# A paged hybrid decoder step on one core: the order of work at the start of the expert stage

## The reference, cut to what matters

```python
        q = (tb @ wq).reshape(blk, PEER_HEADS, PEER_D_KEY)
        s1 = jnp.einsum('thd,hkd->thk', q[..., :half], keys[:, 0])
        s2 = jnp.einsum('thd,hkd->thk', q[..., half:], keys[:, 1])
        sc1, i1 = lax.top_k(s1, PEER_TOPK)
        sc2, i2 = lax.top_k(s2, PEER_TOPK)
...
        sc, sel = lax.top_k(cand, PEER_TOPK)
        idx = jnp.take_along_axis(cidx, sel, axis=-1)
        g = jax.nn.softmax(sc.astype(jnp.float32), axis=-1)
        act = jax.nn.gelu(jnp.einsum('thkd,td->thk', u[idx], tb), approximate=False)
        wgt = (g * act.astype(jnp.float32)).astype(tb.dtype)
        return jnp.einsum('thk,thkd->td', wgt, v[idx])
```

## Time and profile before

| what | value |
|---|---|
| median of 3 executions | 2105.01 us (2101.08 to 2106.8) |
| the profiled execution's own time | 2099.31 us |
| its span, first to last instruction | 2097.5 us |
| mean granted TensorE clock | 0.823 |
| TensorE busy | 1662.4 us, 79% |
| VectorE busy | 1446.4 us, 69% |
| ScalarE busy | 489.6 us, 23% |
| GpSimd busy | 676.2 us, 32% |
| read from HBM | 733.48 MB, 355 GB/s over the span |

### The profile page before, as it was taken

How to read it: one execution, slowest core, us unless ns; L and a number is a source line. 1 busy time by engine, 2 the same in 40 slices (tenths; PEclk the granted TensorE clock), 3 DMA queues, 4 the chain that set the end, 5 groups by cost and what they waited for, 6 DMA issues and landing times. The chain is left out here.

```text
span 2097.5 us, 29681 instructions
## 1 busy us (share of the span) xinstructions
PE 1662.4 (79%) x10874; PEld 839.5 (40%) x10874; DVE 1446.4 (69%) x3630; ACT 489.6 (23%) x1422; POOL 676.2 (32%) x614
## 2 busy tenths in 40 slices
PE   7999999878787666666699999998787776666665
PEld 6888677433333111111178876764332321111110
DVE  3557544778778878778736565347887888787787
ACT  2346211211211221111222543112112112111112
POOL 0011000354544454444300110014444454444442
PEclk9999999887887676666799999998887876666667
DMA  5568897999999999999954688978999999999997
GB/s 181 189 205 302 302 393 279 351 397 421 415 421 421 405 421 421 420 417 412 383 175 155 215 323 293 389 288 351 405 417 416 417 420 409 421 421 418 417 415 319
DMA packets 136004, 746.76 MB, mean 356 GB/s; under 512 B 16692, under 2 KB 17309, under 8 KB 57763
## 3 DMA queue, kind: packets, MB, share of 16 engines
q0 software_dynamic: 84416, 587.50, 68.8%
q1 hardware_dynamic: 51442, 157.37, 20.9%
HBM read 733.48 MB, written 11.52 MB: 355 GB/s over the span
## 5 line engine op out<-in xcount | busy, mean ns | idle before, releaser
L1195 PE MATMUL ps<-arena 64*64 64x512 f32 x4096 | 750.6, 832 | 371.0 <-DVE arena L1852 369.4
L2506 POOL DMA_INDIRECT arena<-in_peer_uv,arena x528 | 628.3, 1190 | 777.4 <-PE ps L1195 619.5
L1843 DVE CUSTOM_DVE_ANT_0 arena<-arena,h 128x1024 f32<-128x1024 f32 x512 | 627.1, 1225 | 216.0 <-DMA arena<-in_peer_uv,arena 208.9
L1195 PEld LDWEIGHTS ps<-arena 64*64 64x64 f32 x4096 | 140.8, 166 | 919.0 <-DVE arena L1852 864.8
L530 PE MATMUL ps<-ht_tok,wring 128*128 128x264 f32 (+1 forms) x1472 | 346.8, 395 | 4.2 <-DMA wring<-in_w_in 2.8
L2228 ACT ACTIVATE arena<-arena 128x1 f32<-128x1 f32 x528 | 105.2, 203 | 969.9 <-DVE arena L1843 968.3
L530 PEld LDWEIGHTS ps<-ht_tok,wring 128*128 128x128 f32 x1472 | 281.2, 194 | 68.8 <-issue 15.8
L1852 DVE TENSOR_SCALAR arena<-consts,arena 128x64 f32<-128x64 f32 (+1 forms) x528 | 164.6, 312 | 38.8 <-ACT arena L2228 35.3
L530 PE MATMUL ps<-arena,wring 128*128 128x264 f32 x256 | 63.9, 393 | 3.2 <-DVE arena L1522 3.2
L530 PE MATMUL ps<-ht_tok,arena 128*128 128x264 f32 (+2 forms) x280 | 60.4, 373 | 1.4 <-DVE ht_tok L1715 1.4
L530 PE MATMUL ps<-arena,gate 128*128 128x256 f32 x256 | 59.1, 383 | 0.0
(11 more groups left out here) (388 smaller groups left out, 1738.2 us busy)
## 6 DMA issues: line engine op xcount, KB each, us to landing
arena<-in_pages SPq DMA_DIRECT2D x256, 272.0 KB, 6.2
wring<-in_w_in SPq DMA_DIRECT2D x36, 1024.0 KB, 5.1
arena<-in_peer_uv,arena POOLq DMA_INDIRECT x528, 12.5
h<-in_state_ssm POOLq DMA_DIRECT2D x16, 512.0 KB, 6.4
out<-h POOLq DMA_DIRECT2D x16, 512.0 KB, 6.1
wring<-in_w_ssm_proj SPq DMA_DIRECT2D x8, 1024.0 KB, 11.4
arena<-in_w_out SPq DMA_DIRECT2D x8, 1024.0 KB, 8.7
arena<-in_peer_wq SPq DMA_DIRECT2D x6, 1024.0 KB, 10.6
```

The costliest lines, as they stand in the source:

```text
L1195: last = pe.matmul(ps[to:to + 64, SUM_BANK[t] + i, :], diag[rows, n % DIAGS, 0:64], ring[rows, HOME[n % RING], cols], start=n in TILE_FIRS ...
L1843: dve.tensor_tensor_reduce(ring[:, HOME[k], 0:D_MODEL], ring[:, HOME[k], 0:D_MODEL], tokens, 1.0, 0.0, ALU.mult, ALU.add, dots[:, column(n ...
L2506: pool.indirect_dma_start(ring[:, HOME[k], :], None, table, bass.IndirectOffsetOnAxis(ap=idx[:, TOPK * u + j:TOPK * u + j + 1], axis=0)).t ...
```

## The change

It rearranges the start of the expert stage; the arithmetic stays the same.

- VectorE does `out(0, 1)` and `sample_gated()` between the two groups of unit 0's search, not behind both.
- The samples' sums on TensorE go behind `outputs(0)`; they used to stand before `out(3, 1)`. For this the sums of a tile get other PSUM banks. VectorE copies `out_samples` in slots 0 and 1 of its loop, and adds `out(2, 1)`, `out(3, 1)` and the samples' sums in slots 2, 3 and 4 (before: 2, 4 and 3, the copies ahead of the loop).
- Head 1's queries go from behind slots 0 and 1 to behind 2 and 3, its scores from 2 to 4, the row turns from 8, 9, 10 to 11, 12, 13, and head 2's queries and scores from 12, 13, 15 to 14, 15, 17.
- Unit 1's experts are found as unit 0's are, in two groups of eight, each published by itself: six steps in slots 8 and 9, four in the next. Unit 2's begin in slot 19 and not 18, with four steps a slot up to slot 31. `px_rows((1, 2))` goes from slot 7 to slot 10.
- GpSimd waits for the second group of unit 1 ahead of slot 24.

```diff
-SUM_BANK = (4, 6, 4)
+SUM_BANK = ((5, 6), (7, 4), (5, 6))
...
-    steps = {0: [("queries", 1, 0, 0, P)], 1: [("queries", 1, 1, 0, P)], 2: [("scores", 1, (0,))]}
+    steps = {2: [("queries", 1, 0, 0, P)], 3: [("queries", 1, 1, 0, P)], 4: [("scores", 1, (0,))]}
     for first in range(3):
-        steps[8 + first] = [("rows", first)]
+        steps[11 + first] = [("rows", first)]
...
-        at = (2, 6, 10) if hh > 2 else (12, 13, 15)
+        at = (2, 6, 10) if hh > 2 else (14, 15, 17)
...
             out(2, 1)
-            pe.wait_ge(sem("aux_free"), since("aux_free") + 4 + marks["sums"])
-            for half in range(2):
-                b = aux.fill()
-                aux.filled(pe.matmul(ps[0:SAMPLES, b, :], cst("sel8"), hp[2][:, half * 512:(half + 1) * 512], start=True, stop=True))
             out(3, 1)
             marks["x", 1] = aux.n
+
+            def samples_summed():
+
+                pe.wait_ge(sem("aux_free"), since("aux_free") + 4 + marks["sums"])
+                for half in range(2):
+                    b = aux.fill()
+                    assert b not in SUM_BANK[0]
+                    aux.filled(pe.matmul(ps[0:SAMPLES, b, :], cst("sel8"), hp[2][:, half * 512:(half + 1) * 512], start=True, stop=True))
+                marks["x", 2] = aux.n
...
             for n in range(SLOTS):
                 outputs(n)
+                if n == 0:
+                    samples_summed()
...
-            def first_experts():
+            def early_experts(u):
...
-                    first_rows(k, n)
+                    yield
+                    yield from eight_rows(u, k, n)
+                    yield
                     if k == 0:
                         for half in range(2):
                             last = dve.match_replace(halves[half], top[:, at[half]], halves[half], -3e38)
                         then(last)
+                        yield "first found"
...
-            first_experts()
-            out(0, 1)
-            sample_gated()
+            for said in early_experts(0):
+                if said == "first found":
+                    out(0, 1)
+                    sample_gated()
             out(1, 1)
-            ahead = best_experts(1)
-            for half in range(2):
-                copy4(hp[2][:, half * 512:(half + 1) * 512])
+            ahead = early_experts(1)
 
             def late_tiles(n):
 
-                if n == 2:
-                    out(2, 1)
-                elif n == 3:
+                if n < 2:
+                    copy4(hp[2][:, n * 512:(n + 1) * 512])
+                elif n < 4:
+                    out(n, 1)
+                elif n == 4:
...
-                elif n == 4:
-                    out(3, 1)
-                elif n == 6:
+                elif n == 7:
                     px_mean(1, slice(46, 48))
-                elif n == 7:
+                elif n == 10:
                     px_rows((1, 2))
...
-                for _ in range(0 if n < 7 or n in (TOPK, TOPK + 1) else 4 if n < 12 else 3):
+                for _ in range(0 if n < 8 or TOPK <= n < TOPK + 3 else 6 if n < 10 else 4 if n < 2 * TOPK else 3):
                     next(ahead, None)
...
                 if n == 5:
-                    act.wait_ge(sem("aux_free"), since("aux_free") + 4 + marks["x", 1])
+                    act.wait_ge(sem("aux_free"), since("aux_free") + 4 + marks["x", 2])
...
-                for step in STEPS.get(n - 2 if n >= 8 else n - 4, ()):
+                for step in STEPS.get(n - 2 if n >= 8 else n - 3, ()):
...
-                if n in (0, TOPK // 2):
+                if u < 2 and n % (TOPK // 2) == 0:
                     pool.wait_ge(sem("idx_ready"), since("idx_ready") + 1 + n // (TOPK // 2))
                 elif j == 0:
-                    pool.wait_ge(sem("idx_ready"), since("idx_ready") + u + 2)
+                    pool.wait_ge(sem("idx_ready"), since("idx_ready") + u + 3)
```

More of the change, by code:

```diff
@@ L1194, in outputs @@
                             rows, to = slice(64 * i, 64 * i + 64), 64 * ((i + half) % 2)
-                            last = pe.matmul(ps[to:to + 64, SUM_BANK[t] + i, :], diag[rows, n % DIAGS, 0:64], ring[rows, HOME[n % RING], cols],
+                            last = pe.matmul(ps[to:to + 64, SUM_BANK[t][i], :], diag[rows, n % DIAGS, 0:64], ring[rows, HOME[n % RING], cols],
                                              start=n in TILE_FIRST, stop=n in TILE_LAST, skip_group_check=True)
                         continue
-                    last = pe.matmul(ps[32 * half:32 * half + SAMPLES, SUM_BANK[t] + half, :], diag[:, n % DIAGS, 0:SAMPLES], ring[:, HOME[n % RING], cols],
+                    last = pe.matmul(ps[32 * half:32 * half + SAMPLES, SUM_BANK[t][half], :], diag[:, n % DIAGS, 0:SAMPLES], ring[:, HOME[n % RING], cols],
                                      start=n in TILE_FIRST, stop=n in TILE_LAST, skip_group_check=True)
@@ L1722, in first_rows @@
                 then(dve.tensor_scalar(iw[:, TOPK + 8 * k:TOPK + 8 * k + 8], ctopi[:, eight], wide - 1, None, ALU.bitwise_and))
+                yield
                 then(dve.tensor_copy(split(sel), split(iw)))
+                yield
                 picks = hot[:, 256:256 + 16 * wide].rearrange("p (s i j) -> p s i j", s=2, j=wide)
                 then(dve.tensor_tensor(picks, bc(split(sel), 3, wide), bc(bc(cst("iota")[:, 0:wide], 1, 8), 1, 2), ALU.is_equal))
+                yield
                 then(dve.tensor_tensor(picks, picks, bc(topf.rearrange("p (s j) -> p s j", s=2)[:, :, 0:wide], 2, 8), ALU.mult))
+                yield
                 then(dve.tensor_reduce(split(sel), picks, AX.X, ALU.add))
-                dve.scalar_tensor_tensor(out=idx[:, 8 * k:8 * k + 8], in0=sel[:, 8 * k:8 * k + 8], scalar=float(N_KEYS),
+                yield
+                at = TOPK * u + 8 * k
+                dve.scalar_tensor_tensor(out=idx[:, at:at + 8], in0=sel[:, 8 * k:8 * k + 8], scalar=float(N_KEYS),
                                          in1=sel[:, TOPK + 8 * k:TOPK + 8 * k + 8], op0=ALU.mult, op1=ALU.add).then_inc(sem("idx_ready"), 1)
-            def first_experts():
-                dve.wait_ge(sem("scores_out"), since("scores_out") + SCORES_AT[0, 0])
-                halves = [keysc[:, 0, 0, half, :] for half in range(2)]
+            def early_experts(u):
+                dve.wait_ge(sem("scores_out"), since("scores_out") + SCORES_AT[u, 0])
+                halves = [keysc[:, u, 0, half, :] for half in range(2)]
                 grid = lambda ap, n: ap.rearrange("p (i j) -> p i j", i=n)
@@ L1863, in tile_sum @@
                             rows, at = slice(64 * i, 64 * i + 64), 64 * ((i + half) % 2)
[L1864 removed]
+                            last = dve.tensor_tensor(x[rows, t, cols], x[rows, t, cols], ps[at:at + 64, SUM_BANK[t][i], :], ALU.add)
                         continue
                     dve.wait_ge(sem("last_sums"), since("last_sums") + half + 1)
[L1867 removed]
+                    last = dve.tensor_tensor(x[0:SAMPLES, t, cols], x[0:SAMPLES, t, cols], ps[32 * half:32 * half + SAMPLES, SUM_BANK[t][half], :], ALU.add)
                 last.then_inc(sem("tile_added"), 1)
[L1870 to L1872 removed]
+            for said in early_experts(0):
+                if said == "first found":
+                    out(0, 1)
+                    sample_gated()
             out(1, 1)
[L1874 to L1876 removed]
+            ahead = early_experts(1)
             def late_tiles(n):
[L1880 to L1882 removed]
+                if n < 2:
[3 more added lines that the diff above has]
+                elif n == 4:
                     for half in range(2):
```

15 lines of the change are left out of this document (9 added, 6 removed).

## The result

The changed kernel takes **2112.02 us** (median of 7 executions, 2108.41 to 2114.66), the kernel before on the same chip 2104.2 us (2098.9 to 2106.8). The ratio is put at 1.0042, 95% interval 1.0031 to 1.0054: 8.8 us slower, 6.5 to 11.4 (the two medians lie 7.8 us apart). The span of the profiled execution is 2112.0 us with a mean granted clock of 0.823, as before.

What follows compares the result with a forecast made beforehand. DMA paces the later slots, but compute delays slot 31's starved gather at each expert stage's start. Layer 0 +5.7 and layer 1 +4.3 make +10.0 us: profiled 2099.3 becomes 2109.3, median 2115.0; range 2096 to 2122.

Steps and rivals of the forecast that it cites:

- Case C: The forecast itself and dearer forms: late turns and queries at half clock delay slot 31's gather; 2108 to 2122, chance 0.53.
- The last starved gather sets the price: Expert-stage start: the price per layer is how much slot 31's gather moves, 5.7 us later in layer 0.
- The 12.5 us from outputs(11) on at half clock: TensorE after diagonal(11): four slots' outputs and three turns take 12.5 us, so head 2's first product starts at 419.5.
- The clock's return 3.5 us into the first product: Head 2's first product on TensorE: full clock back at 423, making the product 5.6 us long.
- The rule on transposes: TensorE's row turns: transposes do not count as busy for the clock like other matmuls, so turns keep it low.
- Layer 1: Second layer's slot 31 gather: the same +5.7 us, less 1.4 of DMA work left, makes +4.3.
- Head 3's second product: TensorE ahead of outputs(23): 4.63 us before, taken as 1.1 us longer, at half clock for somewhat over half.
- Rival A: TensorE's clock back early, full from 410: slot 31's gather 1.7 us sooner, time 2101.6; chance 0.27.
- Rival B: Start of expert stages: the dry queue was the loss, 10.4 us of DMA idle time goes, time 2094.6; chance 0.20.

Runs made afterwards that it cites:

- e4: Changed kernel with the row turns of tile 1 and the samples as plain matmuls with the identity instead of transposes; 2126.61 us, ratio 1.0118.
- f3: Kernel before with all three row turns behind slot 8 instead of behind slots 8, 9 and 10; 2098.9 us, ratio 0.9984.
- g3: Changed kernel with its three row turns all behind slot 11 instead of behind 11, 12 and 13; 2109.02 us, ratio 1.0026.
- f1: Changed kernel plus 2, 2, 5 and 1 unread TensorE products ahead of outputs(8), (9), (10) and (11); 2112.4 us, ratio 1.0047.
- f2: Changed kernel with turns, head 2's queries and unit 2's search put back, plus unread products ahead of outputs(8) and (9); 2102.95 us, ratio 1.0.
- f4: Changed kernel with row turns behind slots 9 to 11 and samples' rows behind slot 8, queries still late; 2102.56 us, ratio 1.0008.
- e1: Changed kernel with unit 1's search, px_rows, row turns and head 2's queries as before; gate, sums and head 1's queries kept; 2104.16 us, ratio 1.0006.
- g2: Changed kernel with head 2's queries and unit 2's search put back and the three row turns together behind slot 9; 2095.61 us, ratio 0.9968.
- g1: f4 with its three row turns together behind slot 9; 2104.0 us, ratio 0.9996.

## Why the prediction was right

Forecast 2115.0 us, or +10.0; measured 2112.0 and a ratio that makes +8.8. Case C, with both of the steps that it was built on. After is read as time less 5.0 us, which is how much later its slot 0's gather is.

| step | forecast | after, less 5.0 |
|---|---|---|
| `outputs(0)` | near 378.5 | 377.9 |
| `inputs(8)`, when DMA has the rows | 388.8 | 388.5 |
| slot 16's gather | about 396 | 395.8 |
| `diagonal(11)` ends | 407.0 | 406.8 |
| head 2's first product starts | 419.5 | 419.4 |
| its length, clock back | 5.6 us, at 423 | 5.49 us, at 422.8 |
| scores | 431.6 | 431.4 |
| unit 2's search | 433.4 | 433.3 |
| `diagonal(22)` | 447.6 | 447.5 |
| slot 31's gather, layer 0 | 456.9 (+5.7) | 456.8 (+5.5) |
| slot 31's gather, layer 1 | +5.7, of which 1.4 hidden | +3.5 |

- **The last starved gather sets the price.** Right in kind. The time went up by 8.8 us, the two gathers by 9.0. In e4 they are 13.2 + 9.7 = 22.9 us later than before, and the time +24.8. The runs in which slot 31 comes earlier don't pay back as much: f3 has 8.5 us less in the two gathers and 3.4 in the time (4.9 from the first gather to the end).
- **The 12.5 us from outputs(11) on at half clock** are 12.6 (411.80 to 424.36). The value was taken from the earlier trace rows piece by piece, and every piece has kept its duration.
- **The clock's return 3.5 us into the first product** was a choice between two ends. The rows of after have 3.4. My reason, that the earlier trace rows are the nearest, with turns and outputs in alternation at 0.50, is what f3 and g3 bear out; that the two ends of the choice lay 20 us apart and 3.5 came within 0.1 of 3.4 is in part luck. The rule on transposes that I quoted beside it as agreeing is not: e4 has none and no earlier return.
- **Layer 1** was mis-sized, by two errors that partly cancel: I let the same +5.7 happen there and took 1.4 off for DMA's work in hand. The gather itself moved by only 3.5, and from slot 0's gather to the end it is 3.6 us longer, where I had 4.3: nothing of the 3.5 was hidden. Its clock came back 58.6 us after slot 0's gather, in layer 0 it was 61.6, and layer 0's first product, at half clock for 3.4 us, had it for only 0.9 there.
- **Head 3's second product**, forecast at 4.63 + 1.1, took 5.63 us; good.
- **Rival A** falls: its point of decision was the clock back by 414; it came at 422.8. Its rule from the Trainium skill (TensorE: Matmul & The Clock Gate, Part 1, the table of the two states), full clock again after a stretch of work, is at odds with 411.80 to 424.36, over 12 us without a gap at 0.50. A's sum also halved the turns at full clock; f1 and f2 have them at 1.59 us for 1.91. An estimate with that (four outputs at 1.02 from start to start in f1, turns of 1.59, 1.59 and 1.06) makes 8.3 us at full clock of the 12.5, and not 6.3.
- **Rival B** is half true, and that half is worth knowing: the dry queue of the first 60 us did go, 357 to 398 and 361 to 400 GB/s, 5.9 and 5.6 us by the sum above. It was paid back with interest in the next 60.

One thing that the prediction did not see: it treats the turns' move as a fixed cost of work at half clock. By f4, of the 4.7 us at the scores some 2.8 are the loss of cover, and 1.9 the half clock in outputs and product. Behind slots 9 and 10 a turn stands where TensorE waits for VectorE; behind 11 to 13 it stands where VectorE waits for TensorE.

What stays open. By their DMA loss e1 and f2 should be 5 us faster than before, and were not; the intervals reach to -1.9 and -3.2. In their profiled executions the distance from the first gather to the end is 1.7 and 3.0 us shorter, so some 3 us of the gain are not there even in the same execution; where they go was not traced. And the stretch was never run at full clock: f1 could not hold it there. An estimate from its pieces (outputs at 1.02 us from start to start, turns at 1.59, 0.7 us of waiting as in f1) is 9.0 us for the 12.6, and with the product at 3.83 the scores 5.2 us earlier; no run shows it.

## What to carry to other kernels

Work that fills an engine's waiting time is not free to move: before it is put off, look for the stretch where its engine waits, and price it at nothing there and in full behind it (f4: the turns two slots earlier, 7 us of the 8.8 back). Removing the largest visible wait (8.73 us) gained nothing, because what ends last was another gather; sum what the bottleneck moves over the whole start-up, before and after, rather than one wait. And where TensorE runs at half clock, the order of short jobs matters: the same three turns in a block with outputs in a row behind them gave back 3.4 us at the scores in g3, 2.1 in f3 and 1.9 in g2 against turns strung between outputs, and nothing in g1.

## What the runs showed of the hardware

Of TensorE's clock. It stayed at 0.50 while TensorE was fully busy with 64-row outputs and 128-column turns in alternation: 12.6 us in the changed kernel, over 18 in e4 with plain matmuls alone. In f1 it fell from 1.00 in such a stretch, with waits of 0.7 us in it. Around head 2's first product in layer 0 it came back in every run either in outputs with no turn between them or in that 264-column product: f3 4.0 us after the block of turns ended, e4 2.9 us into the product. In f1 I had expected 1.00 throughout, since TensorE hardly waited.

A plain 128-column fp32 product with the identity took twice as long as the transpose of the same tile, in records and in time: 4.10 us for 12 against 1.91 for 6, both at half clock.

Half the clock did not mean twice the time for every kind of work. One slot's outputs took 1.09 us at 1.00 and 1.98 at 0.50, but a turn of six transposes 1.59 and 1.91.
